# Moving small work off TensorE's way in a fused three-layer transformer kernel

## The reference, cut to what matters

```
# first block
u   = rmsnorm(x, g);  proj = u @ w_in                    # 2336 columns
o_a = gated linear attention (4 heads, both directions)  # keys, values, gates from proj
o_s = banded_window_gqa(qs, ks, vs, sink, rel_table)     # bias = rel_table[t5_buckets(rel)], 3 blocks of keys
h   = x + rmsnorm(concat(o_a, o_s) @ w_out)
h   = h + rmsnorm(square(relu(rmsnorm(h) @ w_up)) @ w_down)       # the MLP, 4096 hidden
# second block, layer 0
q, k, v, ga, u, gb = split(rms_norm(h) @ a_w_in)
ya  = sliding_window_attention(q, k, v, sinks) * silu(ga)         # 8 heads, 2 blocks of keys
yb  = multiscale_pool(u, pool_w, pool_scale) * silu(gb)           # windows 2, 4, 8, 16
h   = h + rms_norm(concat(ya, yb) @ ab_w_out)
# second block, layer 1
a, b, gate = split(rms_norm(h) @ c_w_in)
conv = depthwise causal convolution of a * sigmoid(b), 31 taps    # 1024 channels
y   = silu(layernorm(conv + bias)) * silu(gate)
out = h + rms_norm(y @ c_w_out)
```

## Time and profile before

| what | value |
|---|---|
| median of three runs | 1041.22 us (1037.6 to 1041.86) |
| the profiled execution | 1038.82 us, of it span 1037.0 us |
| TensorE busy | 997.4 us, 96% |
| VectorE, ScalarE, GpSimd busy | 565.3, 397.3, 58.4 us |
| mean granted TensorE clock | 0.992 |
| chain that ended last | 84% TensorE, 9% VectorE, 3% ScalarE, 3% issue, 1% DMA |

### The profile page before, as it was taken

The page is one execution under the profiler, slowest core; times in us unless marked ns, Lnnn a source line. Parts: engine busy times, 40 slices in busy tenths (PEclk is TensorE's granted clock), DMA queues, the critical chain, the costliest instruction groups (busy, mean ns, idle before and its releaser), DMA issues.

```text
span 1037.0 us, 12886 instructions
## 1 busy us (share of the span) xinstructions
PE 997.4 (96%) x5280; PEld 804.2 (78%) x5280; DVE 565.3 (55%) x765; ACT 397.3 (38%) x646; POOL 58.4 (6%) x49
## 2 busy tenths in 40 slices
PE   4999999999999999999999999989889999999997
PEld 3977787878888888888888878768768886677786
DVE  2346766657441343344334483365554766889963
ACT  4235663376333341134133354243463721222551
POOL 2100102000000000000000000013000100000300
PEclk9999999999999999999999999989999999999999
DMA  6832102233222323322224214302041465655121
GB/s 194 154 98 79 41 2 82 96 121 118 100 95 82 121 82 113 131 82 82 82 90 146 90 41 135 126 35 82 1 148 44 128 186 143 171 145 166 50 82 81
DMA packets 63362, 104.84 MB, mean 101 GB/s; under 512 B 3974, under 2 KB 27399, under 8 KB 63176
## 3 DMA queue, kind: packets, MB, share of 16 engines
q1 hardware_dynamic: 62968, 103.77, 31.7%
q10 hardware_dynamic: 336, 0.25, 0.1%
HBM read 99.43 MB, written 4.58 MB: 100 GB/s over the span
## 4 chain that ended last, share of the span: by engine, by line
PE 84%; DVE 9%; ACT 3%; issue 3%; DMA 1%; ACTq 0%; DVEq 0%
PE acc L791 24%; PE acc L792 24%; PE acc L793 24%; PE ps L1076 2%; PE psT L1061 1%; PE psT L950 1%; PE acc L1050 1%; PE psT L929 1%; DVE wlr L1819 1%; DVE psT L2201 1%; DMA hot<-in_onehot_dram 1%; ACT wh L1446 1%; PE ps L950 1%; ACT lg L1528 1%; DVE sm L1937 1%
## 5 line engine op out<-in xcount | busy, mean ns | idle before, releaser
L1819 DVE TENSOR_TENSOR wlr<-wl,wh 128x2048 fp32r<-128x2048 f32 (+1 forms) x66 | 145.2, 2204 | 77.7 <-ACT wh L1446 77.7
L791 PE MATMUL acc<-act_hi,wh 128*128 128x512 f32 x464 | 184.8, 398 | 0.3 <-DVE wlr L1819 0.3
L793 PE MATMUL acc<-act_hi,wlr 128*128 128x512 f32 x464 | 181.7, 392 | 0.0
L792 PE MATMUL acc<-act_lo,wh 128*128 128x512 f32 x464 | 181.6, 391 | 0.0
L1446 ACT ACTIVATE wh<-wl 128x2048 fp32r<-128x2048 f32 (+1 forms) x68 | 124.3, 1832 | 58.7 <-DMA wl<-in_w_up_dram 35.7
L791 PE MATMUL acc<-wh,act_hi 128*128 128x512 f32 (+1 forms) x352 | 133.6, 380 | 0.0
L793 PE MATMUL acc<-wh,act_lo 128*128 128x512 f32 (+1 forms) x352 | 130.6, 371 | 0.0
L792 PE MATMUL acc<-wlr,act_hi 128*128 128x512 f32 (+1 forms) x352 | 130.4, 370 | 0.0
L791 PEld LDWEIGHTS acc<-act_hi,wh 128*128 128x128 f32 x464 | 87.9, 189 | 23.1 <-issue 4.2
L793 PEld LDWEIGHTS acc<-act_hi,wlr 128*128 128x128 f32 x464 | 87.6, 189 | 18.7
L792 PEld LDWEIGHTS acc<-act_lo,wh 128*128 128x128 f32 x464 | 87.8, 189 | 17.3
(11 more groups left out here) (237 smaller groups left out, 1422.6 us busy)
## 6 DMA issues: line engine op xcount, KB each, us to landing
wl<-in_w_up_dram SPq DMA_DIRECT2D x16, 1024.0 KB, 6.5
wl<-in_w_down_dram SPq DMA_DIRECT2D x16, 1024.0 KB, 7.3
wl<-in_c_w_in_dram SPq DMA_DIRECT2D x20, 512.0 KB, 4.9
raw<-in_w_in_dram SPq DMA_DIRECT2D x18, 512.0 KB, 4.8
shifted<-glu_dram SPq DMA_DIRECT2D x32, 262.0 KB, 4.7
wl<-in_a_w_in_dram SPq DMA_DIRECT2D x8, 1024.0 KB, 6.2
wl<-in_w_out_dram SPq DMA_DIRECT2D x4, 1024.0 KB, 6.3
wl<-in_ab_w_out_dram SPq DMA_DIRECT2D x4, 1024.0 KB, 7.4
```

The source lines that it names most:

```text
L791: pe.matmul(dst, hi, x_hi, start=first, stop=False)
L792: pe.matmul(dst, hi, x_lo, start=False, stop=False)
L793: return pe.matmul(dst, lo, x_hi, start=False, stop=last)
L1819: dve.tensor_tensor(wlr[slot][:, kk, cols], wl[slot][:, kk, cols], wh[slot][:, kk, cols].bitcast(F32), ALU.subtract).then_inc(wlo_done, 1)
```

## The change

The two small TensorE instructions of the start move into the query projection; VectorE's two copies move behind the first lower parts; ScalarE splits the second weight slot before it copies the turned blocks; SP's queue is reordered. In the second attention query tile 3 and all half tiles move by one unit, upper and lower parts of a weight piece lie in different units, and the pool products are interleaved with the last turn. In the passages of MLP and convolution the order alone changes.

```diff
 # start: TensorE
+                        if half == 0 and (kh, s) == (0, 0):
+                            turn_tables()
...
-            pe.transpose(acc[:, 0, 0:V_N], vec_rows[:, :], ident[0:V_N, 0:V_N]).then_inc(vec_ps, 1)
-            pe.matmul(acc[0:8, 1, :], relw[:, :], hot[:, :], start=True, stop=True).then_inc(relf_ps, 1)
+            def turn_tables():
+                pe.wait_ge(act_lo_done, 2)
+                pe.wait_ge(vec_in, 16)
+                pe.transpose(ps6[:, 0:V_N], vec_rows[:, :], ident[0:V_N, 0:V_N]).then_inc(vec_ps, 1)
+                pe.wait_ge(rel_in, 2 * 16)
+                pe.wait_ge(gatew_set, 1)
+                pe.matmul(ps7[0:8, :], relw[:, :], hot[:, :], start=True, stop=True).then_inc(relf_ps, 1)
...
+                    if b == 2:                      # in turn_first
+                        pe.wait_ge(vec_done, 1)
+                        pe.wait_ge(relf_sb, 1)
 # start: ScalarE
             first_upper(0, 0)
+            first_upper(0, 1)
             first_turned(0)
-            first_upper(0, 1)
             first_turned(1)
 # start: VectorE
             first_normed(0)
             first_normed(1)
             first_lo_turned(0)
             first_lo_turned(1)
+            dve.wait_ge(vec_ps, 1)
+            dve.tensor_copy(vec[:, :], ps6[:, 0:V_N]).then_inc(vec_done, 1)
+            dve.wait_ge(relf_ps, 1)
+            dve.tensor_copy(relF[:, :], ps7[0:8, :]).then_inc(relf_sb, 1)
             first_normed(2)
 # start: SP's queue (masks, restart and gate weights come here, ahead of relF)
             sp.wait_ge(relf_sb, 1)
             sp.dma_start(relF_dram, ...)
+            wait_slot(2)
+            load(0, w_in, KS)
             sp.wait_ge(relf_out, 16)
 # passage out of the MLP: TensorE
-            for b in range(NBLK):
+            for b in range(2):
                 block_turned(1, b)
                 token_tile(N_GA, b, 0)
-                if b < 2:
-                    turn_block(1, b + 2)
+            turn_block(1, 2)
+            for b in range(2):
+                token_tile(N_GA, b, 1)
+            turn_block(1, 3)
+            for b in range(2, NBLK):
+                block_turned(1, b)
+                token_tile(N_GA, b, 0)
                 token_tile(N_GA, b, 1)
 # the same: VectorE (ScalarE's hi_turned moves alike, ahead of pre_scale)
-                    if b >= 2:
+                    if b == 2 or (b == 3 and s != 1):
                         lo_turned(s, b - 2)
...
-                    if b in (1, 2):
+                    if b == 1 or (b == 2 and s != 1):
                         lo(following, b - 1)
+                    if s == 1 and b == 2:
+                        lo_turned(s, 1)
                     if b == NBLK - 1:
                         lo_turned(s, b - 1)
                     normed(s, b)
+                    if s == 1 and b == 2:
+                        lo(following, 1)
 # second attention: the order for all engines
-                     ("wtile", N_Q, 2), ("wsplit", N_U, 1), ("wtile", N_Q, 3)]
-            halves_left = [("wtile", n, m, h) for n in (N_U, N_GB) for m in range(4) for h in range(2)]
-            splits = {2: (N_GB, 0), 3: (N_GB, 1), 10: (N_AO0, 0), 11: (N_AO0, 1)}
-            for k in range(STEPS + 2):
+                     ("wtile", N_Q, 2), ("wsplit", N_U, 1)]
+            halves_left = [("wtile", N_Q, 3)]
+            halves_left += [("wtile", n, m, h) for n in (N_U, N_GB) for m in range(4) for h in range(2)]
+            uppers = {2: (N_GB, 0), 4: (N_GB, 1), 10: (N_AO0, 0), 12: (N_AO0, 1)}
+            lowers = {3: (N_GB, 0), 5: (N_GB, 1), 11: (N_AO0, 0), 13: (N_AO0, 1)}
+            pooled = (4, 7, 9, 12)
+            for k in range(STEPS + 1):
...
-            return steps + [("pool_out", 0)]
+            return steps + [("pool_out", 2), ("pool_out", 3), ("turn", 3), ("pool_out", 0), ("pool_out", 1), ("branches", 0)]
 # in qk: the first unit waits for query tile 1 alone
-                        pe.wait_ge(evD_done, evacs_before(TILE_AT[N_Q, 3 if i == 0 else i], "D") + 1)
+                        pe.wait_ge(evD_done, evacs_before(TILE_AT[N_Q, max(i, 1)], "D") + 1)
 # N_AO0 takes its inputs in the order 0, 1, 2, 3, 6, 7, 4, 5; ScalarE and VectorE make them in it ("branches")
 # convolution: VectorE
-                     (9, 5): (stats, 1, slice(512, 896), 7)}
...
+            stats(1, slice(512, 896), 7)
             chain.link(stats(2, slice(896, 1024), 8))
```

More of the change, by code:

```diff
@@ L562, in mixer2_steps @@
                      ("wtile", N_Q, 0), ("keys_values", 1), ("wtile", N_Q, 1), ("wsplit", N_U, 0),
-                     ("wtile", N_Q, 2), ("wsplit", N_U, 1), ("wtile", N_Q, 3)]
-            halves_left = [("wtile", n, m, h) for n in (N_U, N_GB) for m in range(4) for h in range(2)]
-            splits = {2: (N_GB, 0), 3: (N_GB, 1), 10: (N_AO0, 0), 11: (N_AO0, 1)}
-            for k in range(STEPS + 2):
[L567 to L573, removed]
+                     ("wtile", N_Q, 2), ("wsplit", N_U, 1)]
[5 more added lines that the diff above has]
+            for k in range(STEPS + 1):
+                work = [halves_left[k]]
+                if k in uppers:
+                    work.insert(0, ("upper",) + uppers[k])
+                if k in lowers:
+                    work.insert(0, ("lower",) + lowers[k])
+                if k in (2, 4, 6, 8):
+                    work.append(("pool_window", k // 2 - 1))
+                if k in pooled:
+                    work.insert(0, ("pooled", pooled.index(k)))
                 steps += attention_unit(k, work)
-            return steps + [("pool_out", 0)]
+            return steps + [("pool_out", 2), ("pool_out", 3), ("turn", 3), ("pool_out", 0), ("pool_out", 1), ("branches", 0)]
         def window(layer, n):
@@ L665, in _ @@
             sp.dma_start(sink1[:, :], bass.AP(a["swa_sink"].tensor, 0, [[0, P], [1, 8]])).then_inc(mix1_in, 16)
[L666 to L673, removed]
+            for c, n0 in enumerate((ZA, QA, KA, VA, VA + CW, GA, GA + CW), 3):
                 wait_slot(c)
@@ L1165, in mixer_step_pe @@
                 elif what == "pool_out":
-                    pe.wait_ge(mix2_in, 16 * MIX2_LOADS)
-                    pe.wait_ge(o_done, 8)
-                    pe.wait_ge(vtok_done, 2)
-                    for g in range(4):
-                        pe.wait_ge(pooled_done, g + 1)
-                        dst = (ps6[:, :], ps7[:, :], psT[:, 0, :], psT[:, 1, :])[g]
-                        pe.matmul(dst, pw[:, g, :], uu[:, g, UPAD:], start=True, stop=True).then_inc(yb_ps, 1)
+                    if i == 2:
+                        pe.wait_ge(mix2_in, 16 * MIX2_LOADS)
+                        pe.wait_ge(pooled_done, 4)
+                        pe.wait_ge(pTs_done, 2 * STEPS)
+                    elif i == 0:
+                        pe.wait_ge(oq_done, 2 * STEPS)
+                    elif i == 1:
+                        pe.wait_ge(o_done, 8)
+                        pe.wait_ge(vtok_done, 2)
+                    dst = (ps6[:, :], ps7[:, :], psT[:, 0, :], psT[:, 1, :])[i]
+                    pe.matmul(dst, pw[:, i, :], uu[:, i, UPAD:], start=True, stop=True).then_inc(yb_ps, 1)
             for at, step in enumerate(STEPS_OF[0]):
@@ L1510, in mixer_step_act @@
                     split(i)
-                elif what == "wsplit":
+                elif what in ("wsplit", "upper"):
                     hi(i, step[2])
@@ L1901, in mixer_step_dve @@
                     split(i)
-                elif what == "wsplit":
+                elif what in ("wsplit", "lower"):
                     lo(i, step[2])
```

46 lines of the change are left out of this document (22 added, 24 removed).

## The result

The changed kernel takes 1013.81 us (median of four runs, 1012.97 to 1014.82); the kernel before took 1040.15 beside it (four runs, 1037.6 to 1041.86). The ratio is 0.9745, with a 95% interval of 0.9727 to 0.9764. The profiled execution took 1014.59 us and its span is 1012.8. The forecast was 1014, with a span near 1012.7.

What follows compares the result with a forecast made beforehand. TensorE was taken as the bound, busy 997.4 of 1037.0 us, leaving its idle time and low clock to win. Savings of 5.1 + 1.8 + 16.0 + 1.4 = 24.3 us off 1038.82 gave 1014, range 1010 to 1018 (8 in 10: 1009 to 1022).

Steps and rivals of the forecast that it cites:

- Start: Kernel's start: first query matmul at 15.9 instead of 22.86, saving 5.1 us (bounds 7.0 and 1.7).
- the clock: First query matmuls: 0.7 us allowed for running at 1.2 GHz, between nothing and 4.1 us.
- Rival B: Kernel's start: first query matmuls run slow and block 2's lateness shows, 3.4 us less gain, 1017.5 us; chance 0.09.
- MLP's passage: Passage out of the MLP: both waits before turning blocks 2 and 3 go, saving 1.8 us.
- Second attention: Second attention: waits and low-clock stretches go, saving 16.0 us (bounds 17.6 and 7).
- The 17.6 of the ideal: Second attention: saving if all 11.55 us of waits and 6.0 us of low-clock cost go.
- The 0.7 for one remaining low stretch: Second attention: 0.7 us taken off the saving for one low-clock stretch four times in ten.
- rival A: Second attention: waits go but the clock still falls there, or small stalls return elsewhere; 1021 us, chance 0.14.
- The 0.5 for VectorE beside GpSimd: Second attention: 0.5 us taken off because lower parts of units 5 and 11 come close behind GpSimd's pooling sums.
- Convolution: Convolution's end: the last sum comes 1.93 us earlier, transposes start on time, saving 1.4 us (bounds 1.9 and 0).
- C: Second attention: the denser order is granted only 1.2 GHz throughout, 80 us more than forecast, 1094 us; chance 0.03.
- D: Whole kernel: waits merely change hands, gains sum to below 5 us, 1037 us; chance 0.03.

Runs made afterwards that it cites:

- spare transposes: Changed kernel plus 5 and 6 transposes, their results never read, in TensorE's two gaps at the start: 1012.98 us, ratio 0.9747.
- the start alone: Kernel before with only the start's part of the change: 1034.19 us against 1042.16, ratio 0.9916.
- the last turn ahead: Changed kernel with the second attention's last turn put before all four pool products, as before: 1015.34 us, ratio 0.9768.
- all together without transposes: Changed kernel with block 3 turned earlier, GpSimd's second pooling sum held back, convolution lower parts before the next block's gating product: 1012.51 us, ratio 0.9729.

## Why the prediction was right, step by step

**The sum** was 24.3 us of span and 24.2 were measured. That it fits to 0.1 us is luck: three terms were off by 0.5 to 0.9, and not in one direction. There is luck in the last step too. The forecast was taken from a profiled execution of 1038.82 us, and the profiled execution of the changed kernel took 1014.59 where that gives 1014.5; by the medians the gain was 26.3, not 24.3.

**Start, -5.1 predicted, -4.4 measured between the two profiles.** The chain ahead of the first query matmul was worked out to 15.9 and stands at 15.72; the tables cost 1.13 where 1.15 were set; block 2 was turned without a wait; the bias loads were hidden. What is left is the clock: 0.7 was taken, 1.5 came, and 2.6 in the second profile of the same kernel (1.1 more). I went by the nearest row, 48 fast matmuls behind 3.7 us of transposes, and that row was one draw. The three other profiles with the old start show it. In the kernel with the attention's part alone:

```profile
22.94 0.55 PE L796 MATMUL acc<-act_hi,w_hi 128*128 128x256 f32 x1 [1.94 <-DVE act_lo L2078]
...
39.55 0.39 PE L796 MATMUL acc<-act_hi,w_hi 128*128 128x256 f32 x1 [1.57 <-DVE act_lo L2078]
```

The first token half takes 16.61 us there, and 16.55 and 16.61 with the MLP's and the convolution's part alone, against 15.06 (22.86 to 37.92) in the kernel before: some fifteen slow matmuls, 1.5 us, in three of four profiles of the old start. The slow matmuls of the new start cost 1.4 to 2.6 us in its eight profiles without spare transposes, 1.8 on the average, against 1.15 for the old. The difference is 0.7, the term as predicted, and the second token half starts 5.0 us earlier between the averages (38.9 and 33.9 us, six profiles of the new start in which block 3 is turned where it was). So the 4.4 is low because the one profile of the kernel before was a lucky one, and the 5.1 was about right for a reason that the prediction did not have: it knew of no slow matmuls in the old start. Over the fourteen profiled executions the high clock came for good between 12.35 and 26.9 us; in three with the new start (the start alone, the last turn ahead, all together without transposes) it was high from about 13.6, fell at about 17 and rose again at about 20.4. The Trainium skill (TensorE: Matmul & The Clock Gate, What's actually happening) calls the number of slow matmuls run-variable, and the traces agree: the same start had fifteen of them in one profile and all 24 ahead of the tables in another. Rival B was right in kind and too high in price: of its 3.4 us some 0.8 came at first, and 1.9 in the later profile, in which all 24 matmuls were slow; block 2 was not late.

**MLP's passage, -1.8 predicted, -2.0 measured.** Both waits went, as worked out. The 0.2 lies in the bound given (-2.1), which was put down to the part of a wait that the modelled ends hide; no run tests that.

**Second attention, -16.0 predicted, -16.9 measured.** The cause, VectorE held by ScalarE in one unit, is shown by putting it back (10.2 us lost). The 17.6 of the ideal were reduced by three terms. The 0.4 for the new wait before the first output tile was measured at 0.41. The 0.7 for one remaining low stretch was not needed: none was seen in any of the nine profiled executions with the upper and lower parts in different units, so rival A fell. The 0.5 for VectorE beside GpSimd was about the right size in the wrong place: not the lower parts of units 5 and 11, which had slack, but the gating multiply of unit 4, which TensorE waits for. It cost 0.87 us as a wait, and 0.57 of it could be had back. The reading of the earlier trace rows, that only small copies come late, failed here: the multiply has 512 columns.

**Convolution, -1.4 predicted, -0.9 measured.** The turn of the last channels has no wait, as said. The step that failed is that the statistics lie beside transposes and copy of the last channels, "about as long": the bound "if the mean is then late" came true in part. From the last sum to block 0's lower part (start to start) it takes 12.62 us instead of 11.84. Of these 0.78 us, 0.36 lie in the statistics: what follows them starts 3.34 behind the sum's start instead of 2.98, since VectorE now does all eight in a row where it did half of them before. The other 0.42 lie in the first centring, which takes 1.63 us instead of 1.22 before. It now starts beside the last of a GpSimd subtraction (941.36 to 950.75), which before had ended ahead of it (974.00 against a start at 974.82). That the subtraction is the cause is read from this and from the kernel with the convolution's part alone, which has the same overlap and 1.64; no run takes the subtraction away. TensorE, 1.4 us earlier, waits 0.63 for the lower part behind all this. The remedy was on VectorE: with block 0's lower part ahead of block 1's gating product the wait was gone.

From the changed kernel's timeline:

```profile
941.36 9.39 POOL L1399 TENSOR_TENSOR wlr<-wl,wh 128x2048 fp32r<-128x2048 f32 x2 [26.91 <-ACT wh L1468]
...
947.03 2.70 DVE L2244 BATCH_NORM_STATS2 stat<-convT 128x6 f32<-128x384 f32 x8
...
950.20 1.63 DVE L2276 SCALAR_TENSOR_TENSOR convT<-convT,stat,lng 128x1024 f32<-128x1024 f32 x1
...
957.90 1.23 DVE L2293 TENSOR_TENSOR un<-un,gate 128x1024 f32<-128x1024 f32 x1
...
959.04 1.28 DVE L1887 TENSOR_TENSOR act_lo<-psT,act_hi 128x512 fp32r<-128x512 f32 x2
...
960.38 0.50 PE L797 MATMUL acc<-wh,act_hi 128*128 128x512 f32 x1 [0.63 <-DVE act_lo L1887]
```

**Rivals C and D** fell with the windows: in the changed kernel there is no stretch at 1.2 GHz between 26 us and the span's last few us, and no stretch of waits that took the old ones' place.

What stays open: why the kernel before spreads over 1037.5 to 1044.1 us in one series. Only one of its executions was profiled. The prediction took a good part of that spread for low-clock stretches, and the record speaks against it: the mean granted clock of that series' nine executions is 0.991 or 0.992 throughout, 0.992 at 1037.47 as at 1041.32 us, and 0.001 of clock is about 1 us. The four profiles with the old order of the second attention have the same three low stretches. The slow matmuls at the start, for which the rows mostly print 1.00, make 1.6 us between these profiles; the rest has no explanation here.

## What to carry to other kernels

When two engines share one in-order list of units, do not put a producer on one and its consumer on the other into the same unit if something urgent is queued behind the consumer; one unit's distance was worth 10 us of 17 here. Look at what waits do to TensorE's clock before pricing it: 11.55 us of short waits brought 6 us of slow work with them, and both went together. Judge edits worth under 2 us by the marks of matched instructions rather than by medians, but only in stretches that are alike from profile to profile: here the start moved by 1.6 us with nothing changed in it, and one profile on each side gave 4.4 where the averages give 5.0.

## What was not expected of the hardware

The low clock of the second attention came without a long idle time. The longest single wait of TensorE ahead of it was 2.05 us, in the kernel before at 692.75; in the run with both parts in one unit the low stretch started at 677.38, where waits of 0.32, 0.37 and 0.98 us had come within three us. The page's granted clock says 1.00 for the first 19 us of the changed kernel although eight transposes take 1.97 us there and 1.03 later, so at the start the durations tell the clock and the row does not. Beside GpSimd a multiply of two SBUF tiles took 1.26 us instead of 0.69 and a copy of two columns 1.02 instead of 0.16, and GpSimd's own addition 1.39 instead of 1.06. The rows read as if each waited for the other's instruction to end, however short its own is: GpSimd's first addition ends at 680.95 and the multiply 0.56 later, the copy ends at 682.45 with the second addition (682.43), and in the run that held the sum back GpSimd's product of 16 columns took 2.22 us and ended at 686.72, just behind VectorE's lower part (686.64). That is a reading of these rows; no run was made to test it.
